# Down projections of 12 of 22 hidden tiles by seven products, and two weight sums made by accumulating DMAs

## What is computed

```python
def swiglu(h, w_gate, w_up, w_down):                  # 1024 -> 2816 -> 1024
    return (jax.nn.silu(h @ w_gate) * (h @ w_up)) @ w_down
h = h + 0.5 * swiglu(rmsnorm(h, g[0]), ffn_w_gate[layer, 0], ffn_w_up[layer, 0], ffn_w_down[layer, 0])
u = rmsnorm(h, g[1]); h = h + mixer(u)
h = h + 0.5 * swiglu(rmsnorm(h, g[2]), ffn_w_gate[layer, 1], ffn_w_up[layer, 1], ffn_w_down[layer, 1])
```

## Time and profile before

| | |
|---|---|
| median of three runs | 1823.51 us |
| profiled execution, its span | 1821.0 us |
| TensorE (PE) busy | 99% |
| VectorE (DVE) busy | 74% |
| ScalarE (ACT) busy | 47% |
| GpSimd (POOL) busy | 3% |
| granted TensorE clock, mean | 0.998 |
| share of the 16 DMA engines, SP's queue | 31.3% |

### The profile page before, as it was taken

One profiled execution on the slowest core, in us unless ns is written; L12 is line 12 of the kernel. 1 busy time (PEld: TensorE's weight loads), 2 busy tenths in 40 slices (PEclk: granted clock), 3 DMA queues, 4 the chain that ended last, 5 costly groups with the idle time before them and its releaser, 6 DMA issues.

```text
span 1821.0 us, 32718 instructions
## 1 busy us (share of the span) xinstructions
PE 1801.7 (99%) x13456; PEld 1720.7 (94%) x13456; DVE 1344.8 (74%) x1814; ACT 859.6 (47%) x1404; POOL 53.1 (3%) x68
## 2 busy tenths in 40 slices
PE   8999999999999999999999999999999999999997
PEld 8999999999999999999999999999998899889986
DVE  7766887557778966896798578855656799568954
ACT  8443464335446543554555335534423565335542
POOL 0000000000000000000000000000124000000000
PEclk9999999999999999999999999999999999999999
DMA  5255233341222333233223322333312223332331
GB/s 179 85 96 116 95 115 108 102 135 59 70 70 82 101 99 108 89 105 105 82 93 108 97 98 97 107 112 112 93 59 70 70 82 105 102 106 93 111 111 57
DMA packets 81107, 176.87 MB, mean 97 GB/s; under 512 B 7292, under 2 KB 12700, under 8 KB 80960
## 3 DMA queue, kind: packets, MB, share of 16 engines
q1 hardware_dynamic: 80544, 174.49, 31.3%
q10 hardware_dynamic: 416, 0.29, 0.0%
HBM read 171.35 MB, written 3.41 MB: 96 GB/s over the span
## 4 chain that ended last, share of the span: by engine, by line
PE 96%; DVE 2%; ACT 1%; DMA 0%; SPq 0%; issue 0%; DVEq 0%; ACTq 0%
PE psum L2028 25%; PE psum L2098 13%; PE psum L2100 13%; PE psum L2101 13%; PE psum L2038 7%; PE psum L2037 4%; PE psum L2041 4%; PE psum L2036 4%; PE psum L2040 3%; PE psum L2148 2%; PE psum L2147 2%; PE psum L2149 2%; PE psum L2157 2%; DMA rb_sb<-in_rel_bias 0%; DVE rms L1391 0%; PE psum L2336 0%
## 5 line engine op out<-in xcount | busy, mean ns | idle before, releaser
L2098 PE MATMUL psum<-fh,wh 128*128 128x264 f32 (+1 forms) x1968 | 559.9, 285 | 2.2 <-ACT psum L728 2.2
L2101 PE MATMUL psum<-fh,wl 128*128 128x264 f32 (+1 forms) x1968 | 557.2, 283 | 0.0
L2100 PE MATMUL psum<-fl,wh 128*128 128x264 f32 (+1 forms) x1968 | 556.7, 283 | 0.0
L2098 PEld LDWEIGHTS psum<-fh,wh 128*128 128x128 f32 x1968 | 371.1, 189 | 3.5 <-issue 3.0
L2100 PEld LDWEIGHTS psum<-fl,wh 128*128 128x128 f32 x1968 | 370.9, 188 | 0.6
L2101 PEld LDWEIGHTS psum<-fh,wl 128*128 128x128 f32 x1968 | 369.8, 188 | 0.0
L588 ACT ACTIVATE wh<-raw 128x1024 fp32r<-128x1024 f32 (+2 forms) x194 | 169.2, 879 | 224.1 <-PE psum L2028 172.7
L2028 PE MATMUL psum<-xs,wh 128*128 128x264 f32 (+1 forms) x1504 | 267.3, 297 | 5.0 <-DVE xs L1341 3.5
L1226 DVE TENSOR_TENSOR wl<-raw,wh 128x1024 fp32r<-128x1024 f32 (+2 forms) x193 | 194.7, 1016 | 95.8 <-ACT wh L588 95.1
L2028 PEld LDWEIGHTS psum<-xs,wh 128*128 128x128 f32 x1504 | 213.7, 189 | 15.6 <-issue 5.2
L2038 PE MATMUL psum<-hs,wh 128*128 128x512 f32 x528 | 206.6, 391 | 0.0
(11 more groups left out here) (314 smaller groups left out, 3000.4 us busy)
## 6 DMA issues: line engine op xcount, KB each, us to landing
raw<-in_w_gate_up SPq DMA_DIRECT2D x175, 512.0 KB, 3.7
raw<-in_w_down SPq DMA_DIRECT2D x64, 384.0 KB, 3.2
raw<-in_w_down SPq DMA_DIRECT2D x64, 320.0 KB, 3.0
raw<-in_od_in SPq DMA_DIRECT2D x21, 512.0 KB, 3.5
raw<-in_ev_in SPq DMA_DIRECT2D x18, 512.0 KB, 3.5
raw<-in_ev_out SPq DMA_DIRECT2D x8, 512.0 KB, 3.5
raw<-in_od_out SPq DMA_DIRECT2D x8, 512.0 KB, 3.5
x<-in_x_t SPq DMA_DIRECT2D x8, 264.0 KB, 4.9
```

The costliest lines, as they stand in the source:

```text
L2098: pe.matmul(psum[:, bank, 0:w], wh[:, slot, cols], high_x, start=start and j == 0, stop=False, skip_group_check=True)
L2100: pe.matmul(psum[:, bank, 0:w], wh[:, slot, cols], low_x, start=False, stop=False, skip_group_check=True)
L2101: last = pe.matmul(psum[:, bank, 0:w], wl[:, slot, cols], high_x, start=False, stop=j == 3, skip_group_check=True)
```

## The change

- Each half layer has three passes of 6, 6 and 10 hidden tiles. In the first two, the **down projection is done by seven products** as well: two "down" jobs for each pass, one job for output tiles 2d, 2d+1, 2d+4 and 2d+5, over 6 hidden tiles; a product has 3 tiles instead of 4, and a quarter is 128x768. In half layer 0 the first pass stays ordinary and follows its ordinary gate and up. That is 14 down jobs (2, 4, 4 and 4) and 41 up groups as before; the 10 tiles of the last pass go down the ordinary way.
- The hidden tiles of those passes are stored in the seven forms that the products take (`fold_first`, `fold_a_lows`, `fold_others`, `fold_b_lows` on VectorE, `fold_a_highs`, `fold_b_highs` on ScalarE) instead of two parts.
- **s1 and s3 are made by DMA**: SP loads a11 (for s3) or a21 (for s1) into a slot, then GpSimd issues an accumulating DMA that adds a21 or a22 onto it. a11, a12 and a22 are loaded besides. The VectorE operations `sum_s1`, `sum_s3` are gone. The queue of SP is put in a new order (`group_loads`), and slots move: five raw slots, seven high, five low. The low parts of a22 and a12 are written over their raw quarters; s4 over a11.
- Of a down job, VectorE scales (`upper_rows`, `lower_rows`) and **GpSimd adds the rows to x** (`add_upper`, `add_lower`): four adds of 128x528 for each job.
- p2 of half layer 0 is always divided. The orders on PE, ACT and DVE are new, one for each kind of place (`turn` is the first down job of a pass, `folding` an up group whose tiles are folded, `straight` one of the last pass).

The core of the diff:

```diff
-PASS_F0 = (0, 10)
-PASS_F = (10, 12)
+PASS_F0 = (0, 6, 12)
+PASS_F = (6, 6, 10)
+TURNED = 2
 STD_F = 6
-X0_ROW = 8
-QUARTERS = ("a11", "a21", "a22", "a12")
-RING_FORMS = ("s2", "s1", "s4", "a22")
+X0_ROW = 9
+X0_FIRST = 2
+LANDS = ("s3", "a11", "s1", "a12", "a22")
+RAW_RING = ("a11", "s1", "a12", "a22")
+HIGH_RING = ("s2", "s3", "a22", "s4")
...
+JOBS, GROUP = [], {}
...
+        if (_q, _p) != (0, 0):
+            JOBS += [(_q, _p, "up", _j) for _j in range(PASS_F[_p] // 2)]
+            if _p < TURNED:
+                JOBS += [(_q, _p, "down", _d) for _d in range(2)]
...
+        def weights_of(q, g, i, k):
+            _, p, _, d = JOBS[g]
+            if is_down(g):
+                c0 = (PASS_F0[p] + reach(g) * k) * P
+                return w_dn[q * KT + 2 * d + 4 * i:q * KT + 2 * d + 4 * i + 2, :, c0:c0 + reach(g) * P].rearrange("s p c -> p s c")
+            at = q * CHUNKS_UP + 2 * group_f(g)[i]
+            return w_gu[at:at + 2, :, 512 * k:512 * k + 512].rearrange("s p c -> p s c")
...
+            def group_loads(q):
+                def quarter_load(kind, g):
+                    i, k = {"s3": (0, 0), "s1": (1, 0), "a11": (0, 0), "a12": (0, 1), "a22": (1, 1)}[kind]
+                    freed((kind, g))
...
+                for g in range(first, end):
+                    quarter_load("a12", g)
+                    if enters(g):
+                        quarter_load("a22", g)
+                    if g + 1 < end:
+                        quarter_load("s3", g + 1)
+                    if not enters(g) and leads(g - 1):
+                        quarter_load("a22", g)
+                    if g + 1 < end:
+                        quarter_load("s1", g + 1)
+                    if not enters(g) and not leads(g - 1):
+                        quarter_load("a22", g)
+                    if g + 1 < end:
+                        quarter_load("a11", g + 1)
...
+            def accumulate(g):
+                q = JOBS[g][0]
+                slot = raw_slot("s3", g)
+                pool.wait_ge(raw_in[slot], RAW_COUNT["s3", g])
+                pool.dma_start(landing("s3", g), weights_of(q, g, 1, 0), accum_op=ALU.add).then_inc(s3_added, 16)
+                slot = raw_slot("s1", g)
+                pool.wait_ge(raw_in[slot], RAW_COUNT["s1", g])
+                pool.dma_start(landing("s1", g), weights_of(q, g, 1, 1), accum_op=ALU.add).then_inc(s1_added, 16)
...
+            def add_upper(n, lo):
+                m = 2 * JOBS[n // 2][3] + n % 2
+                pool.wait_ge(a_out, n + 1)
+                pool.tensor_tensor(x[:, m, lo:L], x[:, m, lo:L], (gate, up)[n % 2][:, lo:L], ALU.add).then_inc(rows_added, 1)
...
+                    if g > first and is_down(g - 1):
+                        add_upper(2 * g - 1, lo)
+                        add_lower(2 * g - 1, lo)
+                    if is_down(g):
+                        add_upper(2 * g, lo)
+                        add_lower(2 * g, lo)
...
-            def sum_s3(g):
-                dve.wait_ge(raw_in[raw_slot("a11", g)], RAW_COUNT["a11", g])
-                dve.wait_ge(raw_in[raw_slot("a21", g)], RAW_COUNT["a21", g])
-                if leads(g):
-                    dve.wait_ge(s1_sum, g + 1)
-                    dve.tensor_tensor(raw_quarter("a21", g), raw_quarter("a11", g), raw_quarter("a21", g), ALU.add).then_inc(s3_sum, 1)
-                else:
-                    dve.wait_ge(p5_done if leads(g - 1) else p7_done, 2 * g)
-                    dve.tensor_tensor(ws[:, 5, :], raw_quarter("a11", g), raw_quarter("a21", g), ALU.add).then_inc(s3_sum, 1)
-            def s1_full(g):
-                return ws[:, 5, :] if leads(g) else raw_quarter("a21", g)
...
+                dve.wait_ge(s2_low, g + 1)
+                dve.tensor_tensor(raw_quarter("a11", g), raw_quarter("a12", g), raw_quarter("a11", g), ALU.add).then_inc(s4_sum, 1)
...
+            def upper_rows(n, real):
+                dve.wait_ge(p3_done, n + 1)
+                upper_left(n)
+                dve.scalar_tensor_tensor(out=halves((gate, up)[n % 2], real), in0=rows_a(4 * (n % 2), real), scalar=0.5,
+                                         in1=halves(rms, real), op0=ALU.mult, op1=ALU.mult).then_inc(a_out, 1)
...
+            def fold_others(g, real):
+                j, count = JOBS[g][3], 4 * turned_before(g)
+                dve.wait_ge(b_up, ups_before(g) + 1)
+                dve.tensor_tensor(unfolded(T3, j, real), halves(up2, real)[:, 1, :], halves(up, real)[:, 1, :],
+                                  ALU.subtract).then_inc(fold_summed, 1)
+                dve.wait_ge(fold_summed, count + 2)
+                dve.scalar_tensor_tensor(out=unfolded(T2, j, real), in0=unfolded(T3, j, real), scalar=-1.0,
+                                         in1=halves(up, real)[:, 0, :], op0=ALU.mult, op1=ALU.subtract).then_inc(fold_summed, 1)
+                dve.wait_ge(fold_summed, count + 3)
+                dve.scalar_tensor_tensor(out=unfolded(T4, j, real), in0=unfolded(T2, j, real), scalar=-1.0,
...
+            def turn_group(g, q, real):
+                n = 2 * g
+                c22(n - 1, real)
+                sum_s4(g)
+                c21(n - 1, real)
+                low_s1(g)
+                up_a_out(g - 1, real)
+                up_b_gate(g - 1, real)
+                fold_first(g - 1, real)
+                low_s4(g)
+                fold_a_lows(g - 1, real)
+                fold_others(g - 1, real)
+                low_a12(g)
+                fold_b_lows(g - 1, real)
+                low_a11(g + 1)
+                low_a22(g)
+                low_s3(g + 1)
+                sum_s2(g + 1)
+                c22(n, real)
+                c22(n + 1, real)
+                c21(n, real)
+                low_s2(g + 1)
+                c21(n + 1, real)
+                upper_rows(n, real)
...
+            def product(g, kind, s, x_form, bank, start, real, q=None, js=None):
+                w, count = width(real), reach(g)
+                slot, left = high_slot(kind, g), (raw_low if kind in ("a12", "a22") else wl)
+                left_slot = raw_slot(kind, g) if kind in ("a12", "a22") else low_slot(kind, g)
+                for j in range(count) if js is None else js:
+                    if is_down(g):
+                        pe.wait_ge(fold_low, 2 * (turned_before(g) - count + j) + (1 if x_form in (B11, T1) else 2))
+                        high_x, low_x = folded(x_form, j, 0, real), folded(x_form, j, 1, real)
+                    elif x_form == B21:
+                        high_x, low_x = fl[:, B12, j, 0:w], fl[:, B21, j, 0:w]
+                    else:
...
+            def turn_group(g, q, real):
+                n = 2 * g
+                known, rest = range(reach(g) - 1), (reach(g) - 1,)
+                p4(n - 1, real)
+                p3(n - 1, real)
+                p7(n, real, js=known)
+                p5(n, real, js=known)
+                p1(n, real, js=known)
+                p1(n + 1, real, js=known)
+                p7(n + 1, real, js=known)
+                p1(n, real, js=rest)
+                p5(n + 1, real, js=known)
+                p6(n, real, js=known)
+                p1(n + 1, real, js=rest)
+                p2(n, real, js=known)
+                p6(n + 1, real, js=known)
+                p5(n, real, js=rest)
+                p7(n, real, js=rest)
+                p7(n + 1, real, js=rest)
+                p6(n, real, js=rest)
+                p2(n + 1, real, js=known)
+                p2(n, real, js=rest)
+                p6(n + 1, real, js=rest)
+                p5(n + 1, real, js=rest)
+                p4(n, real)
+                p2(n + 1, real, js=rest)
+                p4(n + 1, real)
+                p3(n, real)
...
+            def folding_group(g, q, real):
+                n = 2 * g
+                p1(n, real)
+                p7(n, real)
+                p3(n - 1, real)
+                p4(n - 1, real)
+                p1(n + 1, real)
+                p6(n, real)
+                p6(n + 1, real)
+                p2(n, real)
+                p5(n, real)
+                p7(n + 1, real)
+                p2(n + 1, real)
+                p3(n, real)
+                p4(n, real)
+                p5(n + 1, real)
```

More of the change, by code:

```diff
@@ new lines, in form, with reach @@
+def form(g):
+    q, p, kind, _ = JOBS[g]
+    if enters(g):
+        return "entry" if q else "first_entry"
+    if leads(g):
+        return "turn"
+    if enters(g - 1):
+        return "after_entry" if q else "after_first_entry"
+    if leads(g - 1):
+        return "after_turn"
+    if ends(g):
+        return "last"
+    if is_down(g - 1):
+        return "up_after_down" if folds(g) else "straight_after_down"
+    return "folding" if folds(g) else "straight"
+def reach(g):
+    return PASS_F[JOBS[g][1]] // 2 if is_down(g) else 4
@@ L968, in _ @@
             std_hidden(2)
-            high_a11(0)
             high(10)
@@ new lines, in straight_group @@
+            def straight_group(g, q, real):
```

(22 more changed lines are left out.)

1565 lines of the change are left out of this document (1041 added, 524 removed).

## The result

The changed kernel takes **1849.6 us** (median of 4 runs, 1848.5 to 1853.6) against 1823.6 for the kernel before. The ratio is **1.0146, 95% interval [1.0132, 1.016]**: it is slower by 26 us, where 1799 and at most 1818 was predicted. The profiled execution has a span of 1848.8 us.

What follows compares the result with a forecast made beforehand. TensorE, 99% busy, was taken as the bound: matmul count times pitch. 1821.0 − 26.1 − 1.3 − 2.2 + 2 + 3 = 1796.4 us of span; with 2.5 for the median, 1799 us. Range: 1793.9 less 2, to 1818.

Steps and rivals of the forecast that it cites:

- Part 1, the matmuls: On TensorE, ordinary down steps removed and seven-product matmuls added: net −26.1 us.
- A: Time of one accumulating DMA, taken as 5.0 us; as a rival, it is slower and sets the pace: 1834 us, 12%.
- bare count: Predicted time from the counted work without any new waits: 1793.9 us, a span of 1791.4.
- Part 2, VectorE and the turns: VectorE's work fits under TensorE's, narrowly in each pass's first down job; 0.3 us charged for each of 7 turns, 2 us.
- its lead of 0.1 to 0.3 us: In a turn, VectorE's results were to be ready this long before TensorE asks for them.
- Part 3, the adds: GpSimd's 56 adds to x hold VectorE operations; bounds 0 to 45 us of VectorE time, 3 us of TensorE time charged.
- rival B: GpSimd's adds hold VectorE in the 7 pairs of down jobs: 32 us at worst, about 1812 us in all, 14%.
- the price of 0.8 us of hold: Time a VectorE subtraction of two SBUF tiles lost beside a GpSimd add: 2.04 us instead of 1.22.
- Part 4, the accumulating DMA: The GpSimd-issued DMAs that make s1 and s3 arrive in time and cost 0 us.
- the thresholds of 8.0 and 6.7: Longest an accumulating DMA may take, in us, before VectorE's sum_s2 waits: in a folding group and in a turn.
- the upper bound of 8.6: Longest time in us assumed possible for an accumulating DMA, from the slowest DMA of the earlier trace.
- the chain: Sequence thought to decide: low_s1, reload of the s1 slot, accumulating DMA, then sum_s2 of the next group on VectorE.

Runs made afterwards that it cites:

- e6: e5 with GpSimd's adds cut to one column and the accumulating DMAs cut to 32 columns (results wrong): 1798.4 us, ratio 0.9864.
- e13: e12 with ScalarE's copies of the up product put ahead of high_s3 and high_a11 in the group after a turn: 1817.75 us, ratio 0.9972.
- e12: e7 with the s3 load for the first group of half layers 0 and 2 issued mid-way through the preceding down projection: 1821.6 us.
- e5: Changed kernel with six of eight table stores issued during half layer 0's first groups, two beside its first two down tiles: 1840.8 us.
- e10: e5 with GpSimd's adds cut to one column, accumulating DMAs whole (result wrong): 1830.3 us, ratio 1.0024.
- e2: Changed kernel with GpSimd's adds cut to one column of each row block (result wrong): 1832.1 us, ratio 1.0035.
- e3: Changed kernel with the adds to x made by VectorE right after each scaling, not by GpSimd: 1845.1 us, ratio 1.0121.
- e7: e5 with the adds to x made by VectorE at places in its list where it was idle: 1825.6 us, ratio 1.001.
- e11: e7 with the accumulating DMAs replaced by plain GpSimd-issued ones of the same bytes (sums wrong): 1803.7 us, ratio 0.9893.
- e8: e5 with GpSimd's adds beside low_a12 moved to VectorE's idle time, and the next group's put ahead of the s1 accumulation: 1840.5 us.
- e1: Changed kernel with the bias table stores moved behind the loads of groups 5 to 8 of half layer 0: 1877.2 us, ratio 1.0292.

## Why the prediction was wrong, point by point

**Part 1, the matmuls: right.** With T, H and A out, the span is 1796.5 us (e6) against a bare count of 1791.4, and 5.1 us are small things: 2.2 of waits, turns that last 18.4 us for 18.2 and groups after them 13.17 for 13.1. The prediction's own 1796.4 agrees to 0.1 us, partly by luck, since it held 3 us for the adds. So with the three costs out the change is worth 25 us; but e6 leaves most of the adds and of the sums out, and no run of the whole computation got further than the 5 us of e13.

**Part 2, VectorE and the turns: right.** All seven turns together wait some 0.5 us, in the changed kernel as in e6; 2 were charged. None lost its lead of 0.1 to 0.3 us, worked out from pitches.

**Part 3, the adds: mis-sized by ten times.** The mechanism was right and the term failed: 3 us were charged; alone they cost 29.4. The bound of 32 us for rival B was right and the choice within it wrong. Two things failed. First, the price of 0.8 us of hold came from one pair of rows, where each engine met the other once; in these groups adds follow each other in GpSimd's list because they queue behind an accumulation (749.78 above), and a VectorE operation that meets two waits 2.05 us. GpSimd loses too, 0.5 to 0.8 us for each add. Secondly, I counted VectorE's slack over the pair (1.9 us), while the holds fall on the two operations that TensorE waits for next. The section "Who interferes with whom" of the page SBUF — State Buffer in the Trainium skill says that the later of the two waits for the whole of the earlier. The trace agrees that whole adds are waited for, and shows more: the operation of 3.00 us ends at 755.5, 0.8 us behind the second add (754.65), as if it had waited for both, though by the profile, whose starts on GpSimd are rough, that one began 0.3 us after it.

**Part 4, the accumulating DMA: wrong on two counts.** It was put at 0 us; alone it costs 31.8. A was taken at 5.0 us. The medians are 6.2 and 5.2, under the thresholds of 8.0 and 6.7. But a median isn't the price at the place that counts: in the group after a turn plain loads go out in the same stretch. There s3 takes 7.3 us in group 19 of the changed kernel, and 9.0 in e12, above the upper bound of 8.6, at a DMA share of 0.96 from 986 to 990 us. And the chain was the wrong one. "s3 has its own slot and is asked for later" was dismissed in a sentence; yet s3 is the first thing that ScalarE asks for, and ScalarE's copies for the current group stand behind it. A wait was followed to its own consumer and not to what is queued behind the waiting instruction. The estimate of 3.2 us from the page DMA: Bandwidth & Descriptors of the Trainium skill (section "Anatomy of one DMA — SWDGE (gpsimd) path") is too short here: 6.2 for these 512 KB with the adding, and 4.9 without.

**Not in the sum at all: the table stores, 8.8 us.** The diff leaves them in `down_loads`. The cost is that of e5 against the changed kernel. The prediction never asked what shares the queue with the loads of the first down projection once its tiles last 4.3 instead of 7.2 us, although a row of 8.6 us for 160 KB was in front of me and served only as a bound for A. DMA room was checked in an up group (0.30), not where the stage had become shorter.

**The clock** was not in the sum either. The changed kernel spends 10.2 us at 1.2 GHz from within the wait of 8.4 us on, and 3.4 behind a later one of 2.1; e10 has four stretches of 3.4 us, behind waits of 3.1, 3.1, 2.2 and 2.5 us. e6, without such waits, has none, and its runs lie within 1.2 us. Where the accumulation is whole and GpSimd's whole adds are gone (e2, e3, e7, e10, e12, e13), the runs spread by 9 to 18 us, and the slower ones have the lower mean clock: in e7 1816.1 us goes with 0.998 and 1834.4 with 0.993. So a wait can cost more than its length. Not each one does: in e5 a wait of 2.2 us at 1006 us is followed by half clock, and two of 2.2 us at 745 and 1660 us are not.

**The rivals** were taken as alternatives. A and B both came true, at 31.8 and 29.4 us alone, and overlapped by 19; their sum lay outside the range because no case held both. A came by another way than its rival had it: `sum_s2` waited only 6.5 us, `high_s3` 41. How A reaches TensorE after a turn is shown by e12 and e13. e13 stays 19 us over e6. Its table has 16.4 us more of waits, 11.5 of them in the groups behind the pairs. By e11 most of this should be A, but how it gets there, and whether another order frees them, was not tried.

## What to carry to other kernels

When an instruction gets a new and slower source, ask first what stands behind it in its engine's list, and price the source at the busiest moment at which it is asked for, not by its usual duration. When a stage is made shorter, everything else that its queue carries is part of the change. Where two suspected costs can hide each other, remove both before believing what each one gives back: here 17.5 and 13.6 us, taken off one at a time, stood for 42 together once the stores were moved.

## What the hardware showed that I had not expected

- An accumulating GpSimd-issued DMA doubles packets and engine time: 29920 and 18.6% against 14944 and 9.8% for the same 54 MB plain. It lands in 6.1 and 5.2 us (medians of 512 and 384 KB in e7) instead of 4.9 and 3.8 (e11), and in up to 10.1 in the changed kernel, beside other transfers. Issuing it occupies GpSimd 1.20 us, a plain one 0.72 (e11).
- A GpSimd add of 128x528 takes 1.11 to 1.31 us beside an idle VectorE (e8), 1.32 where it came first, and 1.8 to 2.1 in group 19 of the changed kernel, beside a busy one. A VectorE subtraction of two SBUF tiles beside two such adds went from 0.95 to 3.00 us.
- Stores from one partition to rows of a DRAM table fill the DMA engines at little bandwidth: at a DMA share of 0.84 the changed kernel, with loads beside them, moves 84 GB/s from 50 to 60 us. In e1, two of them issued just before, it is 27 GB/s at a share of 0.83 to 0.89 from 285 to 291.75 us.
